# A head's weighing four steps later, and GpSimd's dilation-16 copies ahead of the merge

## The reference

```python
for window, dil in DILATED_CONFIGS:          # (128, 1), (512, 4), (2048, 16)
    o, lse = dilated_branch(q, k, v, rel_bias, window, dil)
    outs.append(o); lses.append(lse)
w = jax.nn.softmax(jnp.stack(lses, axis=0), axis=0)
y = jnp.sum(w[..., None] * jnp.stack(outs, axis=0), axis=0)
```

## Time and profile before

| | us |
|---|---|
| median of 3 runs | 1786.97 (1782.43 to 1793.37) |
| profiled execution, its own time | 1789.15 |
| its span | 1787.2 |
| PE / DVE / ACT / POOL busy | 1667.5 / 1174.4 / 800.1 / 330.5 |

### The profile page before, as it was taken

The page is one execution under the profiler, slowest core; times in us unless marked ns, Lnnn a source line. Parts: engine busy times, 40 slices in busy tenths (PEclk is TensorE's granted clock), DMA queues, the critical chain, the costliest instruction groups (busy, mean ns, idle before and its releaser), DMA issues. The chain is left out here.

```text
span 1787.2 us, 27566 instructions
## 1 busy us (share of the span) xinstructions
PE 1667.5 (93%) x9138; PEld 1418.2 (79%) x9138; DVE 1174.4 (66%) x2323; ACT 800.1 (45%) x1993; POOL 330.5 (18%) x207
## 2 busy tenths in 40 slices
PE   5789999999979999999999999998998899949998
PEld 4577888888868888888888888878998898837886
DVE  5531123333218888888888888886886687765996
ACT  3441112222205555555555555557987697732000
POOL 2102100000000000000000000004676476400331
PEclk9899999999989999999999999998998898869999
DMA  4416954566448547554846384418999999656541
GB/s 152 155 59 215 331 219 157 199 203 208 168 124 257 169 154 225 186 173 153 254 153 198 113 249 142 152 51 218 200 216 201 200 217 205 121 166 215 184 142 59
DMA packets 235637, 320.02 MB, mean 179 GB/s; under 512 B 66861, under 2 KB 160488, under 8 KB 232236
## 3 DMA queue, kind: packets, MB, share of 16 engines
q1 hardware_dynamic: 231020, 308.90, 59.3%
q0 software_dynamic: 2400, 9.48, 1.6%
q10 hardware_dynamic: 2080, 0.01, 0.1%
HBM read 208.38 MB, written 109.94 MB: 178 GB/s over the span
## 5 line engine op out<-in xcount | busy, mean ns | idle before, releaser
L1046 ACT ACTIVATE WT_hi<-wt_ps 128x512 fp32r<-128x512 f32 (+1 forms) x320 | 171.1, 535 | 315.9 <-PE wt_ps L978 315.8
L1092 DVE TENSOR_TENSOR_SCAN W<-w,W,zeros 128x512 f32<-128x512 f32 x192 | 248.2, 1293 | 59.2 <-ACT w L1038 58.4
L376 PE MATMUL proj<-h_hi,w_hi 128*128 128x512 f32 x640 | 260.1, 406 | 18.6 <-DVE h_lo L552 15.9
L376 PE MATMUL proj<-h_hi,w_lo 128*128 128x512 f32 x640 | 253.3, 396 | 0.0
L376 PE MATMUL proj<-h_lo,w_hi 128*128 128x512 f32 x640 | 253.0, 395 | 0.0
L1100 DVE TENSOR_TENSOR WT_lo<-wt_ps,WT_hi 128x512 fp32r<-128x512 f32 (+1 forms) x320 | 187.2, 585 | 2.3 <-ACT WT_hi L1046 2.3
L1448 ACT ACTIVATE prob<-neg_s,rows 128x256 f32<-128x256 f32 (+1 forms) x384 | 173.5, 454 | 16.4 <-DVE rows L1508 14.7
L978 PE MATMUL wt_ps<-ident,W 128*128 128x128 f32 x1088 | 173.5, 275 | 6.7 <-DVE WT_lo L1100 5.9
L1038 ACT ACTIVATE w<-z_ps 128x512 f32<-128x512 f32 (+2 forms) x320 | 169.1, 529 | 20.6 <-PE z_ps L968 20.6
L1410 PE MATMUL oa_ps<-va,PT_hi 128*128 128x128 f32 x600 | 158.5, 298 | 18.0 <-DVE rows L1526 18.0
L978 PEld LDWEIGHTS wt_ps<-ident,W 128*128 128x128 f32 x1088 | 131.7, 140 | 43.3 <-DVE WT_lo L1100 15.4
(11 more groups left out here) (157 smaller groups left out, 3498.6 us busy)
## 6 DMA issues: line engine op xcount, KB each, us to landing
wa_hi<-wa_d SPq DMA_DIRECT2D x48, 512.0 KB, 3.8
wa_lo<-wa_d SPq DMA_DIRECT2D x48, 512.0 KB, 5.0
va<-va_d SPq DMA_DIRECT2D x32, 512.0 KB, 11.1
wa_d<-x_sb SPq DMA_DIRECT2D x24, 512.0 KB, 3.9
w_raw<-in_w_tiles SPq DMA_DIRECT2D x18, 512.0 KB, 5.0
moved<-move_d SPq DMA_DIRECT2D x16, 528.0 KB, 4.6
x_sb<-in_x SPq DMA_DIRECT2D x16, 512.0 KB, 5.5
qk_hi_d<-st SPq DMA_DIRECT2D x32, 256.0 KB, 2.9
```

The costliest lines, as they stand in the source:

```text
L376: last = pe.matmul(acc[n % ACC_SLOTS][:], w[w_slot(t)][:, k, :], h[ch][:, k, :], start=(k, a) == (0, 0), stop=(k, a) == (KD - 1, 2))
L1046: act.activation(WT_hi[n % PART_SLOTS][:, cols], t_ps[n % T_SLOTS][:, cols], ACT.Copy) \
L1092: dve.tensor_tensor_scan(W[n % W_SLOTS][:, 0:width][:, ::-1], w[n % W_IN][:, 0:width][:, ::-1], above[:, ::-1], first, ALU.mult, ALU.max). ...
```

## The change

`WEIGH_AT` goes from 4 to 8 and `PAIR_AT` from 13 to 17. `order` takes one dilation at a time, and GpSimd's program calls it for dilation 16 (`ORDER[0]`) ahead of the merge and for dilation 4 (`ORDER[1]`) behind it.

```diff
-    WEIGH_AT, PAIR_AT = 4, 13
+    WEIGH_AT, PAIR_AT = 8, 17
...
-            def order(it, par):
+            def order(it, par, c):
 
                 turn, other = (it, 0) if par == 1 else (at(it, 1, -1), 1)
-                pool.wait_ge(qk_loaded[par], at(it, 16 * HeadTiles.QK_LOADS, 16 * HeadTiles.QK_LOADS * par))
-                for c in ORDER[:2]:
-                    through = max(n for n in range(NB) if BUNCHES[n][0][0][0] == c) + 1
-                    pool.wait_ge(s_done, at(turn, STEPS, other * NB + through))
-                    pool.sem_inc(pool_passed, 1)
-                    heads.order(pool, c, par, ordered)
+                if c == ORDER[0]:
+                    pool.wait_ge(qk_loaded[par], at(it, 16 * HeadTiles.QK_LOADS, 16 * HeadTiles.QK_LOADS * par))
+                through = max(n for n in range(NB) if BUNCHES[n][0][0][0] == c) + 1
+                pool.wait_ge(s_done, at(turn, STEPS, other * NB + through))
+                pool.sem_inc(pool_passed, 1)
+                heads.order(pool, c, par, ordered)
...
-            order(0, 1)
+            order(0, 1, ORDER[0])
+            order(0, 1, ORDER[1])
+            order(1, 0, ORDER[0])
             merge(0, 0)
-            order(1, 0)
+            order(1, 0, ORDER[1])
             with pool.Fori(1, PAIRS - 1) as it:
+                order(it, 1, ORDER[0])
                 merge(it - 1, 1)
-                order(it, 1)
+                order(it, 1, ORDER[1])
+                order(at(it, 1, 1), 0, ORDER[0])
                 merge(it, 0)
-                order(at(it, 1, 1), 0)
+                order(at(it, 1, 1), 0, ORDER[1])
+            order(PAIRS - 1, 1, ORDER[0])
             merge(PAIRS - 2, 1)
-            order(PAIRS - 1, 1)
+            order(PAIRS - 1, 1, ORDER[1])
             merge(PAIRS - 1, 0)
```

## The result

The changed kernel takes 1820.17 us (median of 4 runs, 1818.36 to 1823.7), the kernel before 1786.93 (4 runs). The ratio is 1.019, 95% interval 1.0162 to 1.0218: **slower by 1.9%**. The forecast was 1817 us, range 1796 to 1836.

A forecast was written before the change was run, and what follows sets the result against it. A ring through SP's loads, GpSimd's copies and the merge was to bound the kernel: three odd and three even rings sum to 314.7 us, the output stage begins 30.1 us later, giving 1817 us, range 1796 to 1836.

The forecast's parts named there:

- The ring: Dilated stage: SP's loads, GpSimd's copies, merge, SP's next loads form a loop; 48.0 us in odd heads, 56.9 in even.
- the term taken: From SP's first q and k load to the landing of q's low part: 18.0 us in each head.
- The 1.4 us for gates between the pair's stores: Even heads: the merge also releases the transposes, so gates delay SP's stores by 1.4 us, an estimate.
- Who is held: TensorE stops at step 17 of even heads for the merge, some 6 us, and at step 4 behind odd heads.
- The 15.6 us that VectorE had waited at the minima for nothing shown: Three VectorE waits in the dilated stage, expected to fall mostly inside the new stops; added on top in the upper bound.
- The end: The output stage begins at 1620.5 us, 30.1 us later than before.
- the tail: From head 7's weighing at 1579.2 us to the first load of the output stage: 41.3 us, instead of 52.4.
- the later weighing is a gain taken by itself: Four more steps give 7.1 us of cover for rows returning from DRAM, against a longest wait of 6.6 us.
- rival 4: Worse than the ring: late loads also push the dilation-1 v loads, holding values at step 12; 1840 to 1860 us; 8%.
- Rival 2: Longer heads thin the DMA crowd, so loads land sooner; 1783 us, up to 1798 with the loop's waits; 5%.
- Rivals 1 and 3: 1: the later weighing's cover wins, 1765 us, 5%. 3: waits only change places, 1785 to 1797 us, 10%.

The follow-up runs named there:

- experiment 1: The kernel before with one half of the change each: later steps alone 1801.67 us, ratio 1.0087; copies ahead of the merge alone 1824.5 us, ratio 1.023.
- Experiments 3 and 4: On the changed kernel: 3, q loads ahead of k loads, 1806.99 us; 4, SP's merge wait and dilation-16 read behind dilation-4 writes and values, 1800.55 us.
- experiment 3: Changed kernel with q loads ahead of k loads, a semaphore for each: 1806.99 us, ratio 1.0141; with weighing at step 6, gates at 15 too: 1798.03 us.
- experiment 5: Kernel before plus GpSimd work between maxima and sums of each weighing: two copies 1782.36 us, or four memsets 1782.33 us; each ran once.

## Why the prediction was right

**The ring was the cause, and its terms were.** Forecast 48.0 us for odd and 56.9 for even heads; measured 47.2, 48.2, 46.6 and 56.8, 56.7, 54.9. From the first load to the copy's start it took 16.9 to 18.8 us in the six heads, 18.0 on the mean, which is the term taken. The 1.4 us for gates between the pair's stores did not come: from L1299 to the loads behind it even heads took 19.7, 19.6 and 19.0 us, against the 19.2 of before, so that term was taken 1.2 us too long. The copies' place alone (experiment 1) has the whole loss. Experiments 3 and 4 shortened two terms, and the time followed both times, less than the arithmetic said for reasons that the traces show.

**Who is held** came as said: TensorE at step 17 of even heads for the merge (20.8 us in three, 6 us each forecast), and at step 4 behind odd heads for `k_res` (8.1 us in two). SP's wait at L1297 went to 109.7 us in seven, 15.7 each, within the 10 to 20 per head. The 15.6 us that VectorE had waited at the minima for nothing shown are gone from its waits (L1508, 1215 to 1590 us), as the sum assumed.

**The end was met to 0.4 us through two errors that cancel, which is luck.** Head 7's weighing was to begin at 1579.2 and began at 1575.42, without a wait, as the six rings sum to 310.5 us and not 314.7. From there to the output stage 41.3 us were forecast and 44.7 measured, where the last weighing waits 4.1 us. Its read (L1310, 1599.38) is late since SP stood at L1297 for head 6's merge until 1589.86; the tail was costed without that wait, though it is the same one as in the ring. The output stage begins at 1620.10, forecast 1620.5.

**One step was wrong: that the later weighing is a gain taken by itself.** Experiment 1 has it at 0.9% slower. The step counted the cover for the rows and not the queue behind the merge: five copies and the merge are 30 us, and started at step 9 they end after the next head needs them, with stops of up to 2.7 us. Nor did it price TensorE's slow stretch behind a stop of 2 us, which is most of the loss. The six rings of the forecast did not depend on it, since in the changed kernel the ring is longer than either.

**The rivals.** Of rival 4 the mechanism is there (values late by 14.5 us in four waits) but not its price, 20 us and more above the forecast; that they fall into the slack that the ring leaves is argued from the rings, which did not grow. Rival 2's claim, sooner landings in thinner traffic, is out: the DMA share fell from 1.02 to 0.92, and q's low part landed only 0.8 us sooner at the median (14.0 and 12.6 us after its issue, before 14.8 and 13.4). Rivals 1 and 3 did not come.

## What to carry to other kernels

Before an operation is moved ahead of another in an in-order queue, compare what each waits for: an operation that can start only when a transfer has landed gives its lateness to all that stands behind it, and if one of these releases the queue that issues the transfer, the loop's length, not any engine's load, is the period. Sum the loop from rows and compare it with the present period. And put stores that nobody waits for behind the loads that somebody does, not ahead of them and not at the end of a turn where the next loads queue up: of three places for the same four stores one was 0.6% better and one was no better at all.

## What the runs showed of the hardware that was not expected

**A copy on GpSimd holds back a VectorE operation with two inputs in SBUF until the copy ends.** 0.18 us became 3.60 and 3.52 in the changed kernel, 3.03 and 3.52 in experiment 3, 0.79 beside the shorter copies of experiment 5, and stayed 0.18 beside memsets. The reciprocal with one input was not held (0.25 us at 1269.61 in experiment 3, beside the copy from 1269.55 on), nor were the minima, which read one input from PSUM (0.29 us at 1299.59 in experiment 1, beside a copy from 1296.85 to 1300.82). The Trainium skill states it (SBUF — State Buffer, Who interferes with whom): VectorE takes its second SBUF input through an interface that it shares with GpSimd's reads, and the one that comes second waits for the whole instruction. The traces agree for a VectorE operation that comes second; they add that a chain of such operations waits again at every copy. Whether GpSimd waits where it comes second was not looked at.

**A slow stretch behind a short stop can cost four times the stop.** In experiment 1, TensorE stopped for 2.0 us, was granted 0.50 in the windows at 1297 and 1306 although busy throughout them, and 1.00 at 1318; the four steps of dilation 16 behind the stop took 8.0 us more than before. Where TensorE sets the pace, as in steps of dilation 16, such a stretch nearly doubles the step (4.2 us instead of 2.2).
